# Six products of two units for each output tile in the projections that add to the residual stream, and a wider gap between the halves of their input

## The chip, the cores and the metric

The kernel runs on one core of a Trainium2 chip. The metric is the time of one execution on the device in microseconds (us), taken as the median over several runs. TensorE is called PE below, its weight loads PEld, VectorE DVE, ScalarE ACT, GpSimd POOL, and SyncE SP.

## The reference, cut to what matters

One inference step of a two-layer decoder for two groups of requests that share the weights: a prompt of 256 tokens and 8 sampled tokens, so that every activation has 264 columns. Layer 0 has a Mamba-2 mixer, layer 1 a windowed attention; each is enclosed by two half feed-forwards and followed by a gated embedding.

```python
x = x + 0.5 * swiglu(rmsnorm(x, ffn1_norm), ffn1_wi, ffn1_wo)   # 1024 -> 2816 -> 1024
x = x + mixer_or_attention(rmsnorm(x, mix_norm))                # ends in ssm_out or w_o
x = x + 0.5 * swiglu(rmsnorm(x, ffn2_norm), ffn2_wi, ffn2_wo)
gate = sigmoid(rmsnorm(x, ple_norm) @ ple_gate)
x = x + gate * (p @ ple_proj)
```

## The kernel before, in words

Activations lie transposed: 128 features on the partitions, 264 tokens along the row. The residual stream `x` is 8 such tiles. Every product is made in three parts of a shorter float type: a weight tile is split into `whi` and `wlo`, an activation tile into a high half (`xh`, `hh`) and a low half (`xl`, `hl`), and a product is high weight by high input, high weight by low input, low weight by high input (`split_products`, L503 to L509).

The weights are a list of 369 **units** of 128 x 1024 floats (512 KB), used in order, with a ring of four slots for each of `raw`, `whi` and `wlo`. SP loads unit u + 8 into `raw` once `lo_ready` says that unit u + 4 is split. ACT rounds `raw` to `whi` (L1088) when the slot's last user on PE is done, which `unit_used` tells; DVE makes `wlo` by subtraction (L1563) and raises `lo_ready`; PE waits for `lo_ready` before a unit's first product. In the code of ACT and DVE the call `ahead(stage, i, j)` makes the unit that is four further on than unit j of the stage.

There are two kinds of stages. In an **A stage** (first feed-forward matrix, query, gate, Mamba input) a unit gives one output tile: 24 products into one PSUM bank. In a **B stage** (`f1o0`, `sout`, `f2o0`, `f1o1`, `o`, `f2o1`: the second feed-forward matrix, the Mamba output and the attention output) a unit is one tile of the input, `hh[:, kt, :]` and `hl[:, kt, :]`, for all 8 output tiles: `unit_b` (L744) makes three products into each of the 8 banks in turn, and all banks keep accumulating over the stage. `stage_b` (L779) runs the first unit alone (in `sout` the first three units are done by `sout_part`, in pieces), then a loop of four units a turn, then single units, and the last two units together with six products for each bank, so that the banks become ready one after the other (`b_done`). The feed-forward stages have 22 units, `sout` 16, `o` 8.

At the end of a B stage DVE's `add_b` (L1585) adds the banks to `x` (L1593), ACT's `split_x` (L1132) makes `xh` (L1123) and the squares `sq` (L1126), DVE makes `xl` (L1582), and POOL's `add_squares` (L2189) adds the eight squares one by one, from the second on. PE has gone on with the first two units of the next A stage, `unit_pair` (L544), which waits for `xl` tile by tile and, ahead of the eighth tile, makes the column sums of the squares (L542, in the query stage L539), for which POOL's last addition has to be done. DVE and ACT have orders of their own: ahead of `add_b` DVE makes the `wlo` of the next stage's first two units, units n and n + 1 counted from the B stage's start, which take the slots of units n - 4 and n - 3.

In `sout` DVE's order for j = 0 to 13 is: `wlo` of unit j + 4, then for j = 2 to 9 `normed(j + 6)` (L1961), then for j = 4 to 11 `low_z(j + 4)` (L1945), which is the low half of input tile j + 4. In `f1o1` DVE has the key normalisation (L1721, L1723, L1716) between the `wlo` of units 3 and 4.

Of the kernel before, what the change touches and what calls it, by code (L numbers as in the profile page):

```python
# [22 lines left out]
P = 128  # L23
D = 1024
KT = D // P
T = 256
SEQS = 8
N = T + SEQS
# [8 lines left out]
RING = 4  # L37
UNIT = KT * P
HALF = UNIT // 2
WARM = 30  # L40
PAD = 16
LOW = FT * N + PAD
SCALE = 64 ** -0.5

# [4 lines left out]
U0 = {}  # L49
# [118 lines left out]
def trunk_kernel(nc, weights, xT, g1, pT, cst, vec, convst, ssm0, kcT, vc_in, ck, cv,  # L168
# [3 lines left out]
    with ExitStack() as ctx:  # L172
# [322 lines left out]
        def _(pe):  # L495
# [8 lines left out]
            def split_products(out, w, tile, rh, rl, start, stop):  # L504

                c = slice(tile * P, tile * P + P)
                pe.matmul(out, whi[:, w, c], rh, start=start, stop=False)  # L507
                pe.matmul(out, whi[:, w, c], rl, start=False, stop=False)  # L508
                return pe.matmul(out, wlo[:, w, c], rh, start=False, stop=stop)  # L509
# [234 lines left out]
            def unit_b(stage, u, s, kt, where, order, first, hready):  # L744
# [22 lines left out]
                    mm = split_products(bank[m][:, 0:N], s, m, rh, rl, first, False)  # L767
                mm.then_inc(unit_used, 1)

            def sout_part(j, tiles, last=False):  # L770

                pe.wait_ge(lo_ready, U0["sout"] + j + 1)
                pe.wait_ge(hl_ready, HREADY["sout"] + j + 1)
                for m in tiles:
                    mm = split_products(bank[m][:, 0:N], (U0["sout"] + j) % RING, m, hh[:, j, :], hl[:, j, :], j == 0, False)
                if last:
                    mm.then_inc(unit_used, 1)

            def stage_b(stage, n, after, begun=0):  # L779
# [4 lines left out]
                    begun = 1  # L784
                loops = (n - 2 - begun) // RING
                with pe.Fori(0, loops) as i:
                    for j in range(begun, RING + begun):
                        u, _, s = unit(U0[stage], i, j)
                        unit_b(stage, u, s, i * RING + j, after, range(8), False, i * RING + (h0_ + j + 1))
                for j in range(begun + loops * RING, n - 2):  # L790
                    u, _, s = unit(U0[stage], 0, j)
                    unit_b(stage, u, s, j, after, range(8), False, h0_ + j + 1)

                pe.wait_ge(lo_ready, U0[stage] + n)
                pe.wait_ge(hl_ready, h0_ + n)
                for m in range(KT):
                    for j in (n - 2, n - 1):
                        mm = split_products(bank[m][:, 0:N], (U0[stage] + j) % RING, m, hh[:, j, :], hl[:, j, :], False, j == n - 1)
                    if m < KT - 1:
                        mm.then_inc(b_done, 1)  # L800
                mm.then_inc(unit_used, 2)

            def embed(stage, layer):

# [1758 lines left out]
```

## Time and profile before

| | |
|---|---|
| median of 3 runs | 1190.88 us (1190.69 to 1191.04) |
| the profiled execution's own time | 1190.14 us |
| its span, first to last instruction | 1188.3 us |
| PE busy | 1179.1 us, 99% of the span, 9769 matmuls |
| PE weight loads busy | 1152.0 us, 97% |
| DVE busy | 869.6 us, 73% |
| ACT busy | 699.6 us, 59% |
| POOL busy | 248.3 us, 21% |
| granted TensorE clock | 1.00, the higher of its two levels |

A matmul's row gives its start and the time to its modelled end, about 0.28 us, but the next one starts after about 0.12 us, since they are pipelined. So what a product costs is read from the starts of the first of one stretch and the first of the next, divided by the count, not from the busy time.

### The profile page before, as it was taken

To read this page: it belongs to the slowest core of one execution; us is meant where nothing else is said; L and a number is where in the kernel's file an instruction comes from. 1 tells how busy PE (TensorE), PEld (TensorE's weight loads), DVE (VectorE), ACT (ScalarE), POOL (GpSimd) and SP (SyncE) were. 2 spreads that over 40 slices of the span, in tenths; PEclk is the share of its full clock that TensorE was granted. 3 is DMA by queue.
4 is the path that set the end of the run, shared out by engine and by line. 5 is a ranking of instruction groups with operands and counts; after the bars stand their busy time and mean duration, and the time that the engine had idled before them with its cause. 6 is when DMAs were issued, how large, how long until landed. Compare 5 with 4: busy or idle time off the path is not lost.

```text
span 1188.3 us, 26506 instructions
## 1 busy us (share of the span) xinstructions
PE 1179.1 (99%) x9769; PEld 1152.0 (97%) x9769; DVE 869.6 (73%) x1377; ACT 699.6 (59%) x1149; POOL 248.3 (21%) x352
## 2 busy tenths in 40 slices
PE   9999999999999999999999999999999999999998
PEld 8999999998989899999999999999999899999998
DVE  7767646999899768686745987788468877676448
ACT  6454435787786647555546765555368765444345
POOL 1000002412222202132354333232026310000001
PEclk9999999999999999999999999999999999999999
DMA  8765554755446375877887577656743346555552
GB/s 288 263 198 184 183 177 142 265 185 194 156 148 196 103 224 185 316 225 252 277 292 245 208 271 273 228 170 234 261 155 108 103 164 210 183 184 182 177 180 87
DMA packets 63297, 239.90 MB, mean 202 GB/s; under 512 B 7672, under 2 KB 9632, under 8 KB 58848
## 3 DMA queue, kind: packets, MB, share of 16 engines
q1 hardware_dynamic: 56880, 197.83, 49.9%
q0 software_dynamic: 6064, 40.66, 9.4%
q8 instruction: 41, 0.67, 0.2%
q10 hardware_dynamic: 288, 0.54, 0.2%
q14 instruction: 24, 0.20, 0.0%
HBM read 226.87 MB, written 13.39 MB: 202 GB/s over the span
## 4 chain that ended last, share of the span: by engine, by line
PE 93%; DVE 4%; ACT 1%; issue 1%; DMA 0%; POOL 0%; SPq 0%; DVEq 0%; ACTq 0%; POOLq 0%
PE bank L507 29%; PE bank L508 29%; PE bank L509 29%; PE bank L877 1%; PE bank L872 1%; DVE wlo L1563 1%; DVE xl L1582 1%; PE bank L900 1%; ACT whi L1088 0%; DMA raw<-weights 0%; PE bank L929 0%; ACT under L1481 0%; PE bank L685 0%; PE bank L671 0%; PE bank L886 0%
## 5 line engine op out<-in xcount | busy, mean ns | idle before, releaser
L1563 DVE TENSOR_TENSOR wlo<-raw,whi 128x1024 fp32r<-128x1024 f32 x367 | 457.9, 1251 | 235.4 <-ACT whi L1088 234.0
L507 PE MATMUL bank<-xh,whi 128*128 128x264 f32 x2008 | 576.1, 287 | 1.4 <-DVE xl L1767 0.6
L508 PE MATMUL bank<-xl,whi 128*128 128x264 f32 x2008 | 569.2, 283 | 0.0
L509 PE MATMUL bank<-xh,wlo 128*128 128x264 f32 x2008 | 568.8, 283 | 0.0
L1088 ACT ACTIVATE whi<-raw 128x1024 fp32r<-128x1024 f32 x367 | 385.5, 1055 | 241.1 <-PE bank L509 224.3
L507 PEld LDWEIGHTS bank<-xh,whi 128*128 128x128 f32 x2008 | 378.3, 188 | 5.2 <-issue 2.1
L508 PEld LDWEIGHTS bank<-xl,whi 128*128 128x128 f32 x2008 | 378.4, 188 | 0.9
L509 PEld LDWEIGHTS bank<-xh,wlo 128*128 128x128 f32 x2008 | 376.6, 188 | 0.0
L507 PE MATMUL bank<-hh,whi 128*128 (+1 forms) x896 | 255.3, 285 | 0.0
L509 PE MATMUL bank<-hh,wlo 128*128 (+1 forms) x896 | 254.7, 284 | 0.0
L508 PE MATMUL bank<-hl,whi 128*128 (+1 forms) x896 | 254.4, 284 | 0.0
L507 PEld LDWEIGHTS bank<-hh,whi 128*128 128x128 f32 x896 | 169.0, 189 | 1.2 <-issue 0.8
L508 PEld LDWEIGHTS bank<-hl,whi 128*128 128x128 f32 x896 | 169.0, 189 | 0.1
L509 PEld LDWEIGHTS bank<-hh,wlo 128*128 128x128 f32 x896 | 168.6, 188 | 0.0
L1154 ACT ACTIVATE hh<-gu 128x264 fp32r<-128x264 f32 (+1 forms) x88 | 37.4, 425 | 170.1 <-DVE gu L1622 170.1
L2189 POOL TENSOR_TENSOR sq<-sq 128x264 f32<-128x264 f32 x49 | 39.7, 811 | 447.7 <-ACT sq L1126 442.4
L1610 DVE TENSOR_TENSOR gu<-bank,rstd 128x264 f32<-128x264 f32 x192 | 81.9, 428 | 15.6 <-PE bank L509 13.0
L1627 DVE TENSOR_TENSOR hl<-gu,hh 128x264 f32 (+1 forms) x88 | 42.6, 484 | 28.7 <-ACT hh L1154 28.7
L2338 POOL TENSOR_TENSOR xact<-xact,da_bc 128x512 f32<-128x512 f32 x32 | 38.2, 1195 | 100.5 <-PE bank L509 93.1
L1837 DVE SCALAR_TENSOR_TENSOR xact<-under,vs,xact 128x256 f32<-128x256 f32 x96 | 47.3, 492 | 2.3
L1622 DVE TENSOR_TENSOR gu<-gu 128x264 f32<-128x264 f32 x88 | 44.1, 501 | 0.0
L2343 POOL TENSOR_TENSOR xact<-xact 128x512 f32<-128x512 f32 x20 | 31.6, 1579 | 57.7 <-PE bank L509 53.9
(333 smaller groups left out, 1009.5 us busy)
## 6 DMA issues: line engine op xcount, KB each, us to landing
raw<-weights SPq DMA_DIRECT2D x367, 512.0 KB, 3.6
under<-ssm POOLq DMA_DIRECT2D x8, 1024.0 KB, 6.5
xact<-ssm POOLq DMA_DIRECT2D x8, 1024.0 KB, 7.6
out_ssm_s<-xact POOLq DMA_DIRECT2D x8, 1024.0 KB, 5.8
xact<-dtx_rows POOLq DMA_DIRECT2D x5, 1024.0 KB, 10.7
zs<-dtx_rows POOLq DMA_DIRECT2D x2, 1024.0 KB, 15.0
x<-xT SPq DMA_DIRECT2D x4, 264.0 KB, 5.2
xact<-stat_rows POOLq DMA_DIRECT2D x2, 528.0 KB, 6.4
```

The lines of the kernel that those rows point to most:

```text
L507: pe.matmul(out, whi[:, w, c], rh, start=start, stop=False)
L508: pe.matmul(out, whi[:, w, c], rl, start=False, stop=False)
L509: return pe.matmul(out, wlo[:, w, c], rh, start=False, stop=stop)
L1088: act.activation(whi[:, s, :], raw[:, s, :], ACT.Copy).then_inc(hi_ready, 1)
L1154: act.activation(dst, gu[:, 2 * p + 1, :], ACT.Copy).then_inc(hh_ready, 1)
L1563: dve.tensor_tensor(wlo[:, s, :], raw[:, s, :], whi[:, s, :].bitcast(F32), ALU.subtract).then_inc(lo_ready, 1)
L1610: dve.tensor_tensor(dst, src[:, 0:N], rstd[:, :], ALU.mult).then_inc(a_free, 1)
L1622: dve.tensor_tensor(gu[:, 2 * p + 1, :], gu[:, 2 * p, :], gu[:, 2 * p + 1, :], ALU.mult).then_inc(h_ready, 1)
L1627: dve.tensor_tensor(one(hl), gu[:, 2 * p + 1, :], one(hh).bitcast(F32), ALU.subtract).then_inc(hl_ready, 1)
L1837: dve.scalar_tensor_tensor(out=out, in0=xr[:, k:k + T], scalar=vs[:, V_CW + CT * k + c:V_CW + CT * k + c + 1], in1=out, op0=ALU.mult, op1= ...
L2189: pool.tensor_tensor(sq3[:, 0, :], sq3[:, 0, :], sq3[:, m, :], ALU.add).then_inc(sq_pair, 1)
L2338: pool.tensor_tensor(by_head(part), by_head(part), da_bc[:, 2 * k:2 * k + 2, 4 * q:4 * q + 4].unsqueeze(3).to_broadcast([P, 2, 4, 64]), AL ...
```

## The change

`pair_b` takes two units at once: it waits until the second of them is split and both input tiles are there, makes six products for each of the 8 banks (high weights by both high tiles, high weights by both low tiles, low weights by both high tiles) and hands back both slots with the last product (`unit_used` by 2). `stage_b` uses it two times a turn of its loop, for the rest of the units, and for the last two; where the rest is odd, one unit of the old kind comes first. In a feed-forward stage the order is unit 0, pairs 1-2 to 15-16, unit 17, pairs 18-19 and 20-21; in `sout` pairs 3-4 to 9-10, unit 11, pairs 12-13 and 14-15; in `o` unit 0, pairs 1-2 and 3-4, unit 5, pair 6-7. `PAD`, the number of floats between `hh` and `hl`, goes from 16 to 32, so all tiles that are allocated after it lie 64 bytes further on. Nothing else changes; on DVE, ACT, POOL and SP the instructions and their order are the same.

```diff
--- before.py
+++ after.py
@@ -38,7 +38,7 @@
 UNIT = KT * P
 HALF = UNIT // 2
 WARM = 30
-PAD = 16
+PAD = 32
 LOW = FT * N + PAD
 SCALE = 64 ** -0.5
 
@@ -767,6 +767,25 @@
                     mm = split_products(bank[m][:, 0:N], s, m, rh, rl, first, False)
                 mm.then_inc(unit_used, 1)
 
+            def pair_b(u, s, kt, hready, last=False):
+
+                pe.wait_ge(lo_ready, u + 2)
+                pe.wait_ge(hl_ready, hready)
+                hidden = (lambda t, j: t[:, kt + j, :]) if isinstance(kt, int) else (
+                    lambda t, j: t[:, bass.ds(kt + j, 1), :].rearrange("p a n -> p (a n)"))
+                highs, lows = [hidden(hh, j) for j in range(2)], [hidden(hl, j) for j in range(2)]
+                for m in range(KT):
+                    c = slice(m * P, m * P + P)
+                    for j in range(2):
+                        pe.matmul(bank[m][:, 0:N], whi[:, (s + j) % RING, c], highs[j], start=False, stop=False)
+                    for j in range(2):
+                        pe.matmul(bank[m][:, 0:N], whi[:, (s + j) % RING, c], lows[j], start=False, stop=False)
+                    for j in range(2):
+                        mm = pe.matmul(bank[m][:, 0:N], wlo[:, (s + j) % RING, c], highs[j], start=False, stop=last and j == 1)
+                    if last and m < KT - 1:
+                        mm.then_inc(b_done, 1)
+                mm.then_inc(unit_used, 2)
+
             def sout_part(j, tiles, last=False):
 
                 pe.wait_ge(lo_ready, U0["sout"] + j + 1)
@@ -784,21 +803,17 @@
                     begun = 1
                 loops = (n - 2 - begun) // RING
                 with pe.Fori(0, loops) as i:
-                    for j in range(begun, RING + begun):
+                    for j in range(begun, RING + begun, 2):
                         u, _, s = unit(U0[stage], i, j)
-                        unit_b(stage, u, s, i * RING + j, after, range(8), False, i * RING + (h0_ + j + 1))
-                for j in range(begun + loops * RING, n - 2):
+                        pair_b(u, s, i * RING + j, i * RING + (h0_ + j + 2))
+                rest = begun + loops * RING
+                if (n - rest) % 2:
+                    u, _, s = unit(U0[stage], 0, rest)
+                    unit_b(stage, u, s, rest, after, range(8), False, h0_ + rest + 1)
+                    rest += 1
+                for j in range(rest, n, 2):
                     u, _, s = unit(U0[stage], 0, j)
-                    unit_b(stage, u, s, j, after, range(8), False, h0_ + j + 1)
-
-                pe.wait_ge(lo_ready, U0[stage] + n)
-                pe.wait_ge(hl_ready, h0_ + n)
-                for m in range(KT):
-                    for j in (n - 2, n - 1):
-                        mm = split_products(bank[m][:, 0:N], (U0[stage] + j) % RING, m, hh[:, j, :], hl[:, j, :], False, j == n - 1)
-                    if m < KT - 1:
-                        mm.then_inc(b_done, 1)
-                mm.then_inc(unit_used, 2)
+                    pair_b(u, s, j, h0_ + j + 2, j == n - 2)
 
             def embed(stage, layer):
 
```

On PE, at the entry of `sout`'s loop, the order before is this (the loop begins at the branch; `bank`, `hh` and `whi` are the program's names, and a row is one instruction or several alike):

```order
L507 MATMUL bank<-hh,whi 128x264 [waits hl_ready,lo_ready]
L508 MATMUL bank<-hl,whi 128x264
L509 MATMUL bank<-hh,wlo 128x264
L786 UNCONDITIONAL_BRANCH
L786 ISA
L746 REGISTER_ALU [waits lo_ready]
L507 ISA [waits hl_ready]
L507 MATMUL bank<-hh,whi 128x264
L508 REGISTER_ALU
L508 MATMUL bank<-hl,whi 128x264
L509 MATMUL bank<-hh,wlo 128x264
```

And this is the same place after the change:

```order
L509 MATMUL bank<-hh,wlo 128x264
L805 UNCONDITIONAL_BRANCH
L805 ISA
L773 REGISTER_ALU [waits lo_ready]
L780 ISA [waits hl_ready]
L780 MATMUL bank<-hh,whi 128x264
L780 ISA
L780 MATMUL bank<-hh,whi 128x264
L782 REGISTER_ALU
L782 MATMUL bank<-hl,whi 128x264
L784 MATMUL bank<-hh,wlo 128x264 x2
```

The one wait on `lo_ready` ahead of the first product now asks for unit 4 of the stage, where it asked for unit 3.

On PE, at the seam between the last pair of `f1o0` and the A stage behind it, the changed order is this:

```order
L780 MATMUL bank<-hh,whi 128x264 x2
L782 MATMUL bank<-hl,whi 128x264 x2
L784 MATMUL bank<-hh,wlo 128x264 x2
L507 MATMUL bank<-xh,whi 128x264 [waits b_free,lo_ready,a_free,xl_ready]
L508 MATMUL bank<-xl,whi 128x264
```

Before, it was this:

```order
L507 MATMUL bank<-hh,whi 128x264
L508 MATMUL bank<-hl,whi 128x264
L509 MATMUL bank<-hh,wlo 128x264
L507 MATMUL bank<-xh,whi 128x264 [waits b_free,lo_ready,a_free,xl_ready]
L508 MATMUL bank<-xl,whi 128x264
```

The last pair's products are regrouped, and what waits behind them is the same; the slots of the two units ahead of that pair are handed back together, where it was one by one.

## Rows read from the trace of the kernel before

**Rows 1.** The page, the chain that ended last: share of the span by engine.
```profile
PE 93%; DVE 4%; ACT 1%; issue 1%; DMA 0%; POOL 0%; SPq 0%; DVEq 0%; ACTq 0%; POOLq 0%
```

**Rows 2.** Stretches: us, PE busy (matmuls that touch it), clock, DMA share, GB/s.
```profile
137.13:201.29 64.16, 64.16 (x530) 1.00 0.56 180
464.94:581.02 116.08, 116.08 (x964) 1.00 0.75 262
581.02:586.86 5.84, 5.84 (x51) 1.00 0.74 252
```

**Rows 3.** PE in time: start us, us, what; first products of units 4, 5, 7, 8 of f1o0.
```profile
148.78 0.29 PE L507 MATMUL bank<-hh,whi 128*128 x1
...
151.75 0.28 PE L507 MATMUL bank<-hh,whi 128*128 x1
...
157.58 0.29 PE L507 MATMUL bank<-hh,whi 128*128 x1
...
160.47 0.28 PE L507 MATMUL bank<-hh,whi 128*128 x1
```

**Rows 4.** PE in time: last pair of f1o0 and the next stage; two transposes; warm-up.
```profile
195.47 0.29 PE L507 MATMUL bank<-hh,whi 128*128 128x264 f32 x1
...
201.29 0.28 PE L507 MATMUL bank<-xh,whi 128*128 128x264 f32 x1
...
301.56 0.27 PE L849 MATMUL bank<-cs,xact 128*128 128x128 f32 x1
301.67 0.27 PE L850 MATMUL bank<-cs,xact 128*128 128x128 f32 x1
...
1.28 5.54 PE L502 MATMUL bank<-hh 128*128 128x264 f32 x30 [1.28 <-DVE hh L1761]
```

**Rows 5.** A unit handed back at 186.72, from PE over ACT to DVE.
```profile
186.72 0.28 PE L507 MATMUL bank<-hh,whi 128*128 128x264 f32 x1
...
186.92 1.06 ACT L1088 ACTIVATE whi<-raw 128x1024 fp32r<-128x1024 f32 x1 [1.86 <-PE bank L509]
...
188.01 1.23 DVE L1563 TENSOR_TENSOR wlo<-raw,whi 128x1024 fp32r<-128x1024 f32 x1 [1.69 <-ACT whi L1088]
```

**Rows 6.** Entry of sout's loop: PE's unit 3, ACT's and DVE's unit 4.
```profile
414.83 0.28 PE L507 MATMUL bank<-hh,whi 128*128 x1
...
414.39 2.96 ACT L1088 ACTIVATE whi<-raw 128x1024 fp32r<-128x1024 f32 x3 [2.29 <-PE bank L509]
...
415.48 1.23 DVE L1563 TENSOR_TENSOR wlo<-raw,whi 128x1024 fp32r<-128x1024 f32 x1 [1.55 <-ACT whi L1088]
```

**Rows 7.** sout: PE's unit 10 begins, then DVE makes unit 13 and tile 13.
```profile
435.27 0.29 PE L507 MATMUL bank<-hh,whi 128*128 x1
...
436.62 1.23 DVE L1563 TENSOR_TENSOR wlo<-raw,whi 128x1024 fp32r<-128x1024 f32 x1 [0.96 <-ACT whi L1088]
...
438.17 0.43 DVE L1945 TENSOR_TENSOR hl<-zs,hh 128x264 fp32r<-128x264 f32 x1
```

**Rows 8.** f1o1: PE's unit 3 begins, and DVE makes unit 4.
```profile
826.46 0.28 PE L507 MATMUL bank<-hh,whi 128*128 x1
...
825.43 1.78 DVE L1563 TENSOR_TENSOR wlo<-raw,whi 128x1024 fp32r<-128x1024 f32 x1
```

**Rows 9.** The seam behind f1o0: DVE, POOL, PE.
```profile
196.76 1.22 DVE L1563 TENSOR_TENSOR wlo<-raw,whi 128x1024 fp32r<-128x1024 f32 x1 [1.69 <-ACT whi L1088]
197.90 0.42 DVE L1593 SCALAR_TENSOR_TENSOR x<-bank,x 128x264 f32<-128x264 f32 x1
...
200.00 6.22 POOL L2189 TENSOR_TENSOR sq<-sq 128x264 f32<-128x264 f32 x7 [147.07 <-ACT sq L1126]
...
206.46 0.61 PE L542 MATMUL bank<-sq,cs 128*128 128x264 f32 x2
```

**Rows 10.** The seam behind sout: POOL's additions, then PE's product over them.
```profile
451.56 6.21 POOL L2189 TENSOR_TENSOR sq<-sq 128x264 f32<-128x264 f32 x7 [34.60 <-ACT sq L1126]
...
457.88 0.44 PE L542 MATMUL bank<-sq,cs 128*128 128x264 f32 x1
```

## The prediction

> **What bounds the kernel now.** I read four views. The chain of work that ended last comes first: PE has 93% of it [rows 1], so any time in which PE stands still lengthens the run, and any time that a product saves shortens it. Next, the stretches of a B stage, an A stage and the embedding product between them [rows 2]: the clock is 1.00 throughout, PE has work all the time, and DMA is busy a half to three quarters, so nothing starves. Dividing by the products gives their real price: `f1o0` 64.16 us / 528 = 121.5 ns, the first matrix of the next feed-forward 116.08 / 960 = 120.9 ns, the embedding 5.84 / 48 = 121.7 ns (the counts in the rows hold a few products more that only touch the stretch). Third, PE in order of time, unit by unit [rows 3]: the price is not one number, for unit 4 takes 151.75 - 148.78 = 2.97 us (123.8 ns a product) and unit 7 160.47 - 157.58 = 2.89 us (120.4 ns), with the same kinds of products and banks, and another input tile. Last, who makes what PE waits for, in time, at the places where the change alters a wait [rows 5 to 10].
>
> **What the change does, part by part.** It removes no product. It regroups 98 units: 20 in each of the four feed-forward stages, 12 in `sout`, 6 in `o`; 98 x 24 = 2352 products. It adds two kinds of waiting: a pair begins only when its second unit is split and its second input tile is there, and the first unit's slot is handed back a unit (2.9 us) later.
>
> *The handing back.* From the first product behind the handed-back unit, ACT starts 0.20 us later and takes 1.06, and DVE starts 1.29 us after it and takes 1.23, so a unit is ready 2.52 us after [rows 5]. Of two units handed back together the second `wlo` starts 1.14 us after the first, because that is what the next instruction on DVE does (196.76 to 197.90, [rows 9]); it is ready after 1.29 + 1.14 + 1.23 = 3.66 us. The next pair takes PE 48 x 121.5 ns = 5.8 us, so inside the loops 2.2 us of cover are left and nothing is lost. Where one unit stands alone (unit 17, in `sout` 11), the pair behind it needs only the first of the two: 2.52 us against 2.92, which holds by 0.4. SP's queue is released by the same `lo_ready` at most 2.9 us later, and loads are eight units ahead: nothing. POOL's later work waits on `unit_used` too, up to 2.9 us more for every other piece, and is off PE's path: nothing. If ACT or DVE were held up by 2 us in a loop, that cover would be gone and PE would wait for the rest.
>
> *A wait at the entry of `sout`'s loop.* PE begins unit 3 at 414.83; pair 3-4 has to wait for unit 4, whose slot PE had in use until 414.1 to 414.4, so that ACT starts at 414.39 and DVE ends at 415.48 + 1.23 = 416.71 [rows 6]. Between a release and PE's product lie 0.11 us (POOL's end at 451.56 + 6.21 = 457.77, product at 457.88 [rows 10]). So PE starts at 416.82: **+2.0 us**. Queued behind it on PE is the whole rest of the run.
>
> *The wait at pair 12-13 of `sout`.* It needs input tile 13, whose low half DVE makes behind unit 13's `wlo` and one more instruction. Today PE begins unit 10 at 435.27, thereby handing back unit 9, and that half is done at 438.17 + 0.43 = 438.60 [rows 7]: 3.33 us. After the change unit 9 comes back when unit 11 begins, and unit 11 alone, 2.9 us, is the cover: 3.33 + 0.11 - 2.91 = **+0.5 us**. Pair 9-10 needs tile 10 behind two such rounds, but has a pair's 5.8 us of cover: nothing.
>
> *The wait at pair 3-4 of `f1o1`.* PE begins unit 3 at 826.46; DVE, late from the key normalisation, has unit 4 ready at 825.43 + 1.78 = 827.21 [rows 8]. 827.32 - 826.46 = **+0.9 us**. The first pairs of `f2o0` and `o` have the next thinnest cover; I count nothing there.
>
> *The seams behind the B stages.* This is the largest term. With 22 units (and with 16) units n - 4 and n - 3 are one pair, so both slots come back when the last pair begins, T = 195.47 in `f1o0` [rows 4]. DVE makes the next stage's units n and n + 1 from these slots before `add_b`. Today it has only n + 1 left by then and starts `add_b` at 197.90, which is T + 2.43 [rows 9]. After the change it has both: T + 1.29 + 1.14 + 1.14 = T + 3.57, that is 1.14 us later. `xh`, the squares and `xl` all hang on this, and POOL's seven additions follow the second square without a gap: 200.00 + 6.22 = 206.22 today, 207.36 then [rows 9]. PE's column sums stand right behind them, at 206.46, and would start at 207.47: +1.0. Behind `sout` the sums already wait today (457.77 to 457.88 [rows 10]), so all 1.14 us show. The seams of `f2o0`, `f1o1` and `f2o1` are built alike, and I take 1.07 for each. In `o` units 4 and 5 are not a pair (unit 5 stands alone), so its seam stays. Sum: 1.0 + 1.1 + 3 x 1.07 = **+5.4 us**. What comes late next are the roots and the takes of the A stage's first units; they shift by the same 1.14 us as PE does, so they add nothing.
>
> *The products themselves.* The new order alternates two input tiles, and with 128 bytes between the halves the low tiles lie 64 bytes off their high ones in every block of 256 bytes. No stage of the trace has this order; bounds from rows: the slowest unit 123.8 ns (+2.3 x 2352 = +5.4 us), the fastest 120.4 (-1.1 x 2352 = -2.6 us). Nearest are today's last pair, which already makes six products for each bank from two tiles, (201.29 - 195.47) / 48 = 121.3 ns [rows 4], the embedding 121.7 and the A stage 120.9 [rows 2]. I take 121.2: -0.3 x 2352 = **-0.7 us**. Fewer bank changes are part of that: an A stage changes banks once in 24 products, a B stage once in three, and they differ by 0.6 ns, so halving the changes is worth less than 1.4 us. The Trainium skill speaks for a larger gain there: TensorE: Matmul & The Clock Gate, section "A second HAM failure mode: psum-queue depth-cycling", holds that cycling through PSUM banks makes PE idle briefly again and again. The trace doesn't agree to that extent, with its 0.6 ns and a clock at 1.00.
>
> The sum: 2.0 + 0.5 + 0.9 + 5.4 - 0.7 = +8.1 us. Made against the profiled execution's own 1190.14 us this is 1198.2; that execution lies 0.74 us under the median shown, so on the median's scale it is **1199.0 us**.
>
> **The rivals.** *The products shorten and PE ends faster than before.* The place is the interplay of a product's reads with the next weight load; the change would have to bring the 2352 products from 121.5 down by more than 8.8 / 2352 = 3.7 ns, to under 117.8. For it: two transposes with loads of their own start 0.11 us apart [rows 4], and the price does depend on the input tile [rows 3], which is what the gap between the halves alters. At 114 ns, midway: -17.6 + 8.8 = -8.8 us, 1182.1 us. Against it: no unit in rows 3 and no stage in rows 2 is under 120.4 ns, whatever tiles it mixes. The Trainium skill, same page, section "Back-to-back issue gap", would give 264 / 2.4 + 2.5 = 112.5 ns for such a product, an estimate by which 9 ns could still be had; the rows show none of it. SBUF — State Buffer, section "Who interferes with whom", says that PE's two read ports are independent, by which the gap would do nothing; rows 3 speak against that. Chance 0.07.
>
> *No difference.* The products come down to between 118.8 and 116.8 ns, and the waits eat it: within 2.4 us of today, 1190.9. Chance 0.07.
>
> *More than forecast.* After 2 us of standing still at `sout`'s entry the clock falls to its lower level. The warm-up, which ran mostly at that level, took 5.54 - 0.28 = 5.26 us for 29 starts [rows 4], where 121.5 ns each would make 3.5: some 1.7 us. Or the products come out like a slow unit's, 122.5 ns: +2.4 instead of -0.7. Together 1199.0 + 4.8 = 1203.8, either alone about 1201 to 1202. Chance 0.12.
>
> *The seams cost less*, because PE's sums have more room than the rows tell, or the second `wlo` is overtaken: without that term +2.7, 1193.6 us. Chance 0.08.
>
> **How the numbers follow.** The forecast has the rest, 0.66, with its own range of 1197 to 1201 (a product between 120.7 and 122.0 ns, and half a microsecond on the waits). The range of 8 in 10 goes from 1194.5 to 1202.5. About 0.2%, 2.4 us, is what a measurement of this kernel can tell from no change: faster 0.07, within it 0.07, slower 0.86.
>
> **What would show it.** In the profile after: PE waiting for `wlo` (L1563) at the entry of `sout`'s loop for about 2 us and in `f1o1` for 0.9, for `hl` (L1945) in `sout` once for 0.5; the column sums (L542, L539) waiting for POOL at five seams for about 1 us each and not behind `o`; DVE's `add_b` beginning 3.6 us after the last pair instead of 2.4; `f1o0` at 528 products in about 64.0 us. It would be wrong if those waits are missing, or if a B stage takes under 62.2 us (117.8 ns a product), which would carry the run below today's.

## The result, and the profile after

The changed kernel takes **1203.67 us** (median of 5 executions, 1202.24 to 1205.70) against 1190.88 (1190.52 to 1192.33) before, measured beside it: 1.0106 times as long, 95% interval 1.0095 to 1.0116. Forecast were 1199.0 us and a range up to 1202.5. The sign and most of the places were right; the size was not, and the median lies above the range.

The profiled execution took 1202.24 us, its span 1200.4, which is 12.1 us over the span of before. In the page, the chain of work that ended last [rows 1] now reads:

```profile
PE 77%; DVE 9%; issue 6%; ACT 5%; POOL 1%; DMA 0%; DVEq 0%; SPq 0%; POOLq 0%; ACTq 0%
```

PE's share of the chain has fallen from 93% to 77%, since the chain now runs through DVE (9% for 4%), ACT (5% for 1%) and the path between them (`issue`, 6% for 1%) at the places where PE waits. That is where the chain runs, not time lost: the run is 1% longer. PE's waits, by what ended them (us in total, times, longest):

```profile
PE bank L780 <- DVE wlo L1578: 3.4, 3, 1.9
PE bank L542 <- POOL sq L2204: 1.5, 3, 0.5
...
PE bank L507 <- DVE xl L1597: 1.0, 1, 1.0
PE bank L542 <- issue: 0.5, 1, 0.5
...
PE bank L539 <- POOL sq L2204: 0.5, 1, 0.5
...
PE bank L780 <- DVE hl L1960: 0.4, 1, 0.4
```

(Behind line 800 all numbers are 15 higher than before: `wlo` L1563 is now L1578, `add_b` L1593 is L1608, POOL's L2189 is L2204.) Line 780 is the first product of a pair, L542 and L539 are the column sums at the seams. One wait more for `wlo` than forecast is there, and one at L507 for `xl`. The stretches of the six B stages, as [rows 2], in the columns us, PE busy, PEld, DVE, ACT, POOL, clock, DMA share, GB/s:

```profile
137.02:201.30 64.28, 64.28 (x530) 64.28 (x529) 28.26 (x31) 24.77 (x28) 0.18 (x1) 1.00 0.52 173
411.54:456.89 45.35, 43.02 (x350) 42.60 (x349) 26.58 (x38) 21.64 (x30) 2.05 (x4) 1.00 0.57 174
592.08:658.39 66.31, 64.72 (x530) 64.31 (x529) 39.10 (x33) 32.21 (x47) 31.41 (x27) 1.00 0.74 264
826.01:891.64 65.63, 64.75 (x531) 64.52 (x530) 33.28 (x33) 25.83 (x31) 4.36 (x6) 1.00 0.62 211
955.34:978.84 23.50, 23.50 (x192) 23.50 (x193) 13.96 (x18) 12.59 (x18) 1.10 (x2) 1.00 0.60 205
1106.96:1171.25 64.29, 64.29 (x530) 64.29 (x529) 28.26 (x31) 24.78 (x28) 0.19 (x1) 1.00 0.52 174
```

Taking the whole run apart at the first product of each B stage and at the first product behind it gives this account of the 12.1 us. The seams lie in the second column, whose last row goes up to PE's last product.

| | B stage, before → after | from its end up to the next B stage, before → after |
|---|---|---|
| start | | 137.13 → 137.02: -0.1 |
| f1o0 | 64.16 → 64.29: +0.1 | 209.08 → 210.24: +1.2 |
| sout | 42.41 → 45.34: +2.9 | 134.08 → 135.20: +1.1 |
| f2o0 | 64.16 → 66.31: **+2.2** | 166.53 → 167.62: +1.1 |
| f1o1 | 64.33 → 65.63: +1.3 | 62.60 → 63.70: +1.1 |
| o | 23.43 → 23.51: +0.1 | 128.12 → 128.12: 0 |
| f2o1 | 64.16 → 64.29: +0.1 | 23.63 → 24.65: +1.0 |

Second column: +5.5 us in five seams and none behind `o`, where 5.4 and none were forecast. One seam in time, as [rows 9], DVE, POOL and PE:

```profile
196.75 2.36 DVE L1578 TENSOR_TENSOR wlo<-raw,whi 128x1024 fp32r<-128x1024 f32 x2 [4.65 <-ACT whi L1103]
199.02 0.77 DVE L1608 SCALAR_TENSOR_TENSOR x<-bank,x 128x264 f32<-128x264 f32 x2
...
201.12 0.77 POOL L2204 TENSOR_TENSOR sq<-sq 128x264 f32<-128x264 f32 x1 [148.31 <-ACT sq L1141]
...
207.42 0.68 PE L542 MATMUL bank<-sq,cs 128*128 128x264 f32 x2 [0.55 <-issue]
```

DVE now makes two `wlo` where it made one, and `add_b` begins at 199.02 instead of 197.90: 1.12 us later, POOL 1.12 later too. The entries of the loops in `sout` and `f1o1` [rows 6, 8] and the wait for tile 13 [rows 7], each with PE's first product behind the wait (`x1` at L780) and the DVE row that ended it:

```profile
416.67 2.36 DVE L1578 TENSOR_TENSOR wlo<-raw,whi 128x1024 fp32r<-128x1024 f32 x2 [1.59 <-ACT whi L1103]
...
418.14 0.39 PE L780 MATMUL bank<-hh,whi 128*128 x1 [1.95 <-DVE wlo L1578]
...
444.52 0.43 DVE L1960 TENSOR_TENSOR hl<-zs,hh 128x264 fp32r<-128x264 f32 x1
...
445.10 0.36 PE L780 MATMUL bank<-hh,whi 128*128 128x264 f32 x1 [0.38 <-DVE hl L1960]
...
833.91 1.78 DVE L1578 TENSOR_TENSOR wlo<-raw,whi 128x1024 fp32r<-128x1024 f32 x1
...
835.93 0.39 PE L780 MATMUL bank<-hh,whi 128*128 x1 [0.88 <-DVE wlo L1578]
```

From the start of the last product ahead of the wait to the first behind it are 2234, 667 and 1155 ns, where products follow each other in about 120; the product after that comes 0.2 us later instead of 0.12. So the terms are 2.2, 0.6 and 1.1 us; forecast were 2.0, 0.5 and 0.9. In `f1o1` the row of `wlo` ends at 833.91 + 1.78 = 835.69 and PE starts at 835.93: 0.24 us from a release to the product, where the prediction took the 0.11 of a seam. In `sout` it is 0.25 (the first of the two `wlo` ends at 417.89 in the trace), at tile 13 0.15.

What was not forecast is `f2o0`. During this stage POOL works on the Mamba states of the sampled tokens in pieces of 512 columns, four multiplications and then four additions for each token (`late_piece`), and each piece is released by a unit that PE hands back. In time, POOL, DVE and PE at its pair 18-19:

```profile
642.96 1.30 POOL L2358 TENSOR_TENSOR xact<-xact 128x512 f32<-128x512 f32 x1
...
643.07 2.27 DVE L1578 TENSOR_TENSOR wlo<-raw,whi 128x1024 fp32r<-128x1024 f32 x1 [2.65 <-ACT whi L1103]
...
645.40 0.39 PE L780 MATMUL bank<-hh,whi 128*128 128x264 f32 x1 [0.59 <-DVE wlo L1578]
```

and at its end:

```profile
652.73 3.50 DVE L1578 TENSOR_TENSOR wlo<-raw,whi 128x1024 fp32r<-128x1024 f32 x2 [4.02 <-ACT whi L1103]
...
652.88 2.27 POOL L2358 TENSOR_TENSOR xact<-xact 128x512 f32<-128x512 f32 x1
...
653.93 2.30 DVE L1578 TENSOR_TENSOR wlo<-raw,whi 128x1024 fp32r<-128x1024 f32 x1
656.16 0.76 DVE L1608 SCALAR_TENSOR_TENSOR x<-bank,x 128x264 f32<-128x264 f32 x2
...
658.39 0.36 PE L507 MATMUL bank<-xh,whi 128*128 128x264 f32 x1 [1.00 <-DVE xl L1597]
```

A `wlo` that takes 1.23 us elsewhere takes 2.3 where it meets one of POOL's additions, and the late `add_b` keeps PE from the first product of `pg0`, the next A stage (the gate of the embedding). The two waits, 882 and 1284 ns from start to start, make 2.0 of the stage's 2.2 us.

### The profile page after: what moved, and what is told of

Its sections match the earlier page's. It is cut to its first block, busy times and chain, and to the rows that moved or that the text cites. A ratio compares the mean times of both kernels' runs of the same rounds, so it can differ in the third digit from the quotient of the medians.

```text
span 1200.4 us, 26427 instructions
## 1 busy us (share of the span) xinstructions
PE 1184.4 (99%) x9769; PEld 1154.4 (96%) x9769; DVE 870.9 (73%) x1377; ACT 695.0 (58%) x1149; POOL 248.4 (21%) x352
## 4 chain that ended last, share of the span: by engine, by line
PE 77%; DVE 9%; issue 6%; ACT 5%; POOL 1%; DMA 0%; DVEq 0%; SPq 0%; POOLq 0%; ACTq 0%
PE bank L507 17%; PE bank L508 17%; PE bank L509 16%; PE bank L780 7%; PE bank L784 7%; PE bank L782 7%; ACT whi L1103 3%; DVE wlo L1578 3%; POOL sq L2204 1%; DVE gu L1637 1%; DVE gu L1625 1%; PE bank L892 1%; PE bank L887 1%; DVE xl L1597 1%; PE bank L915 1%
## 5 line engine op out<-in xcount | busy, mean ns | idle before, releaser
L1578 DVE TENSOR_TENSOR wlo<-raw,whi 128x1024 fp32r<-128x1024 f32 x367 | 461.4, 1269 | 245.4 <-ACT whi L1103 244.1
L507 PE MATMUL bank<-xh,whi 128*128 128x264 f32 x2008 | 577.0, 287 | 1.7 <-DVE xl L1597 1.0
L1103 ACT ACTIVATE whi<-raw 128x1024 fp32r<-128x1024 f32 x367 | 381.5, 1053 | 261.2 <-PE bank L784 168.6
L507 PEld LDWEIGHTS bank<-xh,whi 128*128 128x128 f32 x2008 | 378.2, 188 | 6.5 <-issue 2.8
L780 PE MATMUL bank<-hh,whi 128*128 (+1 forms) x784 | 159.6, 285 | 3.8 <-DVE wlo L1578 3.4
L784 PE MATMUL bank<-hh,wlo 128*128 (+1 forms) x784 | 159.5, 285 | 0.0
L782 PE MATMUL bank<-hl,whi 128*128 (+1 forms) x784 | 159.0, 284 | 0.0
L2204 POOL TENSOR_TENSOR sq<-sq 128x264 f32<-128x264 f32 x49 | 39.8, 811 | 452.6 <-ACT sq L1141 447.3
L780 PEld LDWEIGHTS bank<-hh,whi 128*128 128x128 f32 x784 | 121.4, 188 | 4.6 <-issue 3.8
L784 PEld LDWEIGHTS bank<-hh,wlo 128*128 128x128 f32 x784 | 121.7, 189 | 0.0
L782 PEld LDWEIGHTS bank<-hl,whi 128*128 128x128 f32 x784 | 121.4, 188 | 0.0
L1642 DVE TENSOR_TENSOR hl<-gu,hh 128x264 f32 (+1 forms) x88 | 39.6, 450 | 28.7 <-ACT hh L1169 28.7
```

What stands on the lines that cost most here:

```text
L780: pe.matmul(bank[m][:, 0:N], whi[:, (s + j) % RING, c], highs[j], start=False, stop=False)
L782: pe.matmul(bank[m][:, 0:N], whi[:, (s + j) % RING, c], lows[j], start=False, stop=False)
L784: mm = pe.matmul(bank[m][:, 0:N], wlo[:, (s + j) % RING, c], highs[j], start=False, stop=last and j == 1)
L1103: act.activation(whi[:, s, :], raw[:, s, :], ACT.Copy).then_inc(hi_ready, 1)
L1578: dve.tensor_tensor(wlo[:, s, :], raw[:, s, :], whi[:, s, :].bitcast(F32), ALU.subtract).then_inc(lo_ready, 1)
L2204: pool.tensor_tensor(sq3[:, 0, :], sq3[:, 0, :], sq3[:, m, :], ALU.add).then_inc(sq_pair, 1)
```

## The experiments

All times are compared with runs of the kernel before on the same chip (medians 1190.55 to 1191.13 us). Stage times are read as in the table above.

### The order at the seam

```diff
-                if (n - rest) % 2:
+                while rest < n:
                     u, _, s = unit(U0[stage], 0, rest)
-                    unit_b(...)
-                    rest += 1
-                for j in range(rest, n, 2):
-                    pair_b(u, s, j, h0_ + j + 2, j == n - 2)
+                    if rest == n - 3:
+                        unit_b(stage, u, s, rest, after, range(8), False, h0_ + rest + 1)
+                        rest += 1
+                    else:
+                        pair_b(u, s, rest, h0_ + rest + 2, rest == n - 2)
+                        rest += 2
```

> The changed kernel with one edit: behind its loop a stage takes a pair first and its single unit third from the end, so that units n-4 and n-3 are handed back apart, as before. Theory (the joint hand-back makes VectorE late at the seam): the five seams give back about 5.3 us, and because the pair that follows a single unit is then the last one, so do the wait for tile 13 in sout (0.6), the wait inside f2o0 (0.9) and the late last residual sum behind f2o0 (1.2, with its work on POOL beside it): 1194.3 profiled, median about 1195. What stays is the loop entry of sout (2.2), of f1o1 (1.1) and the products (0.6). If the gaps inside f2o0 have nothing to do with which units are handed back together, it stays at about 1197.5. Rival (the time is in the order of the products, not in the hand-back): over 1200.

Measured: 1198.08 us (1196.62 to 1199.28), 1.0058 [1.0044, 1.0071], 3 us over the expected median. The parts between the stages are back at 209.09, 134.03, 62.58 and 23.58 us: four of the five seams are gone, and nothing but which units are taken and handed back together was touched there, so the joint hand-back is shown as their cause. The waits for tile 13 and at pair 18-19 are gone too. But the fifth seam stays, 167.66 us behind `f2o0`, and `f2o0` takes 64.66, with a gap of 538 ns at its end. The rows say why, though no run tests it: the pair 17-18 still comes back at once, and three of POOL's additions in a row stretch both of the last `wlo`, so that `add_b` starts 4.1 us after the last pair (at 650.24), though its two units came back apart.

```profile
647.55 5.76 POOL L2359 TENSOR_TENSOR xact<-xact 128x512 f32<-128x512 f32 x3 [3.51 <-PE bank L784]
...
649.86 4.54 DVE L1579 TENSOR_TENSOR wlo<-raw,whi 128x1024 fp32r<-128x1024 f32 x2
654.32 0.76 DVE L1609 SCALAR_TENSOR_TENSOR x<-bank,x 128x264 f32<-128x264 f32 x2
```

That is 1.5 of the 3.8 us by which the profiled execution lies over the expected 1194.3. The rest, and 0.5 us that other parts gained, lies in two things: its first B stage began 1.1 us later (138.09), for which no row gives a reason, and `sout` took 46.42 us, longer than in the changed kernel. The stretches of `sout`, from the wait on (same columns as above):

```profile
415.78:418.02 2.24, 0.29 (x4) 0.08 (x2) 1.48 (x2) 2.24 (x3) 1.41 (x3) 1.00 0.24 82
418.02:419.37 1.35, 1.35 (x10) 1.35 (x11) 1.35 (x2) 0.39 (x1) 0.00 (x0) 0.97 0.56 84
419.37:422.67 3.30, 3.30 (x17) 3.30 (x16) 0.67 (x1) 0.00 (x0) 0.00 (x0) 0.50 0.97 169
422.67:425.00 2.33, 2.33 (x20) 2.33 (x20) 0.49 (x1) 0.00 (x0) 0.00 (x0) 0.99 1.02 415
```

The granted clock halves, to 1.2 GHz, some 1.3 us after the wait has ended, and 15 products follow each other at 220 ns. In the profiled execution of the changed kernel it doesn't, behind the same wait:

```profile
419.50:422.80 3.30, 3.30 (x30) 3.30 (x28) 0.66 (x1) 0.00 (x0) 0.00 (x0) 1.00 0.96 166
```

### The order of the products, and the gap

Three kernels. The second experiment keeps waits and hand-back of the pair and puts the products of before between them:

```diff
-                for m in range(KT):
-                    ...
+                    for j in range(2):
+                        for m in range(KT):
+                            mm = split_products(bank[m][:, 0:N], (s + j) % RING, m, highs[j], lows[j], False, False)
                 mm.then_inc(unit_used, 2)
```

> The changed kernel with the products inside a pair in the order of before (all eight banks for one unit, then for the other), but with the pair's waits ahead of it and its hand-back behind it. Theory (waits and hand-back carry the loss, the product order some 0.6 us): 1201.5 profiled, median within 1 us of the changed kernel (1203 +-1), all gaps at their places. Rival (six products into one bank, with changed input tiles, cost more each, and a product in the old order is 121.5 ns): the same gaps, but the stages' mean product goes from 121.75 back to 121.5 ns, which is the 0.6 us. Second rival (the order is what costs): under 1197.

The third is the changed kernel with `PAD = 16`, the fourth the kernel before with `PAD = 32`.

> The changed kernel with 16 numbers (64 bytes) between hh and hl as before. Theory (a product's time goes by the place of its own input tile, in a cycle of eight tiles, and each tile is read equally often): no difference, within 0.6 us of the changed kernel. If the wider gap helped the pairs, this one is slower by up to 1.5 us; if the wider gap is what made the products 121.75 ns where before had 121.5, it is faster by 0.6 us.

> The kernel before with 128 bytes between hh and hl and nothing else. Theory: no difference (1190.9 +-0.6), the mean product 121.5 ns as before, but the low products take the place in the cycle that their shifted start gives them (two tiles of the eight further on). Rival (the gap itself costs or gives): over 1191.6 or under 1190.2.

Measured: 1203.46 us (1202.79 to 1204.77), 1202.71 (1201.88 to 1204.43) and 1191.62 (1191.34 to 1193.66). The second has every wait of the changed kernel at its place, four of them within 0.03 us of its length and the one in `f1o1` 0.17 us longer: the loss is in waits and hand-back, not in the order. The price of the products is under what medians can tell and is read from `f1o0`, where no kernel waits. Its stretch in the second, third and fourth experiment:

```profile
137.66:201.99 64.33, 64.33 (x530) 64.33 (x529) 28.29 (x31) 24.79 (x28) 0.20 (x1) 1.00 0.52 173
```

```profile
139.31:203.34 64.03, 64.03 (x530) 64.03 (x529) 28.32 (x31) 24.84 (x29) 0.25 (x1) 1.00 0.52 174
```

```profile
137.72:202.06 64.34, 64.34 (x531) 64.34 (x530) 30.23 (x34) 26.92 (x31) 1.19 (x2) 1.00 0.55 180
```

Four profiled executions of kernels with the same `f1o0` as the changed one give 64.286 or 64.287 us, so differences of this size can be read. Of what a B stage's products read, the gap moves `hl` alone. With before (64.16) and the changed kernel (64.29) this is a table of two by two: at 64 bytes unit by unit 64.16, in pairs 64.04; at 128 bytes 64.33 and 64.29. So the pairs do help, by 0.12 and 0.04 us a stage, and the wider gap takes 0.17 and 0.25. My "no difference" for the gap is refuted by the stage times of both experiments on it (the medians can hardly tell: 1191.62 is 0.5 us over before, with an interval of 0.9996 to 1.0014), and so is "back to 121.5 ns" in the second: the gap has a price of its own, and at 128 bytes the old order costs 64.33 / 528 = 121.8 ns.

### POOL's additions

```diff
-                    pool.tensor_tensor(part, part, late_b(q)[:, cols], ALU.add).then_inc(late_sum, 1)
+                    wide = 32 if U0["f2o0"] <= late_unit(n) < U0["f2o0"] + FT else 512
+                    pool.tensor_tensor(part[:, 0:wide], ..., ALU.add).then_inc(late_sum, 1)
```

This kernel leaves out most of those sums.

> The changed kernel, in which POOL's additions for the late outputs are 32 columns wide instead of 512 during f2o0 (most of those sums are left out, all else stays). Theory A (the pair hands two units back at once, POOL then has two additions in a row, the second beside VectorE's low parts, and those take 2.2 us instead of 1.2 while it lasts): low parts of 1.2 us all through f2o0, its gaps of 0.88 us at pair 18-19 and 1.28 us at the first product behind it both under 0.3 us, stage 64.3 us instead of 66.3. The gap of 0.8 us behind the first unit of pg0 stays. Theory B (ScalarE's scaling of late outer products between the two high parts of a pair delays the second low part): gaps and stage stay within 0.3 us of the changed kernel's.

Measured: 1201.81 us (1200.78 to 1202.74), 1.0092 [1.0077, 1.0108]. Pair 18-19 and the end of the stage:

```profile
643.76 0.26 POOL L2359 TENSOR_TENSOR xact<-xact 128x32 f32<-128x32 f32 x1
...
643.86 1.23 DVE L1578 TENSOR_TENSOR wlo<-raw,whi 128x1024 fp32r<-128x1024 f32 x1 [2.66 <-ACT whi L1103]
...
653.81 1.22 DVE L1578 TENSOR_TENSOR wlo<-raw,whi 128x1024 fp32r<-128x1024 f32 x1
654.94 0.77 DVE L1608 SCALAR_TENSOR_TENSOR x<-bank,x 128x264 f32<-128x264 f32 x2
```

`f2o0` takes 64.29 us, neither gap is there, and ScalarE still scales its outer products between the two high parts. Theory A holds for the gaps, B falls; but not every `wlo` of the stage is back at 1.2 us: of 22, three still take 2.0 to 2.2 and one 1.5, beside POOL's multiplications, which were left as they were and cost PE nothing here. The seam behind `f2o0` stays (167.62), now an ordinary one. The rows also say how the two engines share. At 642.96 POOL began first and took its usual 1.30 us, and DVE took 2.27, about its own 1.23 and what was left of POOL's; at 652.88 POOL came second and took 2.27, and DVE's next one, which came third, 2.30. They take turns, they don't share. The Trainium skill says so of two inputs in SBUF against a GpSimd instruction that reads SBUF: the second to issue blocks until the first is done (SBUF — State Buffer, "Who interferes with whom"). The trace agrees. In the kernel before, at the end of the stage, the addition (1.29 us) started 0.24 us after the hand-back and the `wlo` 1.11 us after the addition, so that they overlapped by 0.2 us and the `wlo` took 1.27; in pairs there are two of each in a row. The sharing itself could be seen before the change, in the middle of the same stage, where it cost PE nothing:

```profile
619.18 2.05 POOL L2343 TENSOR_TENSOR xact<-xact,zs 128x512 f32<-128x512 f32 x1 [1.61 <-PE bank L509]
...
620.29 2.02 DVE L1563 TENSOR_TENSOR wlo<-raw,whi 128x1024 fp32r<-128x1024 f32 x1 [0.22 <-ACT whi L1088]
```

### The entries

```diff
                     begun = 1
+                if stage in ("sout", "f1o1"):
+                    u, _, s = unit(U0[stage], 0, begun)
+                    unit_b(stage, u, s, begun, after, range(8), False, h0_ + begun + 1)
+                    begun += 1
                 loops = (n - 2 - begun) // RING
...
-                    if rest == n - 3:
+                    if rest == n - 3 or rest == n - 4:
```

> The kernel of the first experiment (single unit third from the end) with unit 3 of sout and unit 1 of f1o1 on their own ahead of the loops, so that their first pairs are 4-5 and 2-3, and the two units behind the loops of these stages are single. Theory: the wait of 2.2 us in sout goes, and the half-rate products behind it with it (1.5 us in that run), the wait of 1.1 us in f1o1 goes; sout takes 42.6 us, f1o1 64.5; time 1198.1 - 5 = 1193 +-0.7, and its executions lie within 1.5 us of each other, where those of the changed kernel are 3.5 apart. Rival (the low parts are late in any order at a loop's entry, and the wait moves to the next pair): sout over 43.5 us and a gap of over 0.8 us at pair 4-5.

Measured: 1194.05 us (1193.70 to 1195.89), 1.0029 [1.0018, 1.0040]. `f1o1` has no gap left (64.61), as expected. In `sout` the wait of 2.2 us became two, of 445 ns at pair 4-5 and 1055 at pair 6-7, and the stage takes 43.97 us: here the rival was half right. So the median lies over the expected 1193.7, and the executions lie 2.2 us apart, not 1.5. The second wait in the profile (the first, shorter one counts as `issue` there):

```profile
PE bank L780 <- DVE wlo L1583: 0.8, 1, 0.8
```

No half-rate products appear behind either in the profiled execution.

### Stages put back

The changed kernel with `f2o0` alone in the stage code of before, unit by unit, and in the other kernel `sout` alone:

```diff
+                if stage == "f2o0":
+                    ...
+                    return
                 loops = (n - 2 - begun) // RING
```

> The changed kernel with f2o0 alone in the order of before (unit by unit). Theory: f2o0 goes from 66.3 to 64.3 us and the gap of 0.8 us behind the first unit of pg0 goes, 3.0 us together: 1203.7 - 3.0 = 1200.7 +-0.8 (the executions differ by what happens behind the wait in sout). Rival (the wait in front of pg0 comes from the stage's place and not from pairs): the gap of 1.28 us at its end stays over 0.6 us.

> The changed kernel with sout alone in the order of before (unit by unit). Theory: in the profiled execution of the changed kernel sout and the seam behind it cost 2.9 and 1.1 us, and in other executions the products behind the wait of 2.2 us run at half rate for 1.1 to 1.6 us; with no wait there, no half-rate stretch and no scatter. Stage 42.5 us, time 1203.7 - 4.0 - 1.5 = 1198.2 +-0.7, executions within 1.5 us of each other. Rival (scatter and the extra 1.4 us of the median come from elsewhere): 1199.7, still over 3 us between executions.

Measured: 1202.54 us (1201.76 to 1202.63) and 1198.83 (1198.19 to 1200.36). `f2o0` is at 64.33 with 166.51 behind it, 3.1 us less in all, as expected. The median is not: it fell by 1.1 us and lies 1.0 over the expected range. Half-rate products in `sout` hide part of the gain in the profiled execution (46.84 us, with a mean granted clock of 0.998), and the other three executions have 0.996. With `sout` in units it takes 42.53 us with 134.06 behind it, 4.0 less, and the median fell by 4.8. The executions lie 2.2 us apart, not the 1.5 expected; the mean granted clock of all five is 0.999 or 1.000.

### Everything mended

The entries' kernel with `f2o0` in units and `PAD = 16`, and the same with `sout` in units as well:

> The kernel e6_entries with f2o0 unit by unit as in e7_f2o0_in_units, and 64 bytes between hh and hl. Theory (every loss was a hand-back or an entry, and six products into one bank are worth 0.2 ns each at that gap, 121.3 for 121.5 ns): stages at or below those of before (64.04 us for 64.16), 1190.9 - 0.5 = 1190.4, within 0.2% of before. Rival (pairs cost something else that the gaps do not show): 1192 or more.

> The kernel e8_all_mended with sout, too, unit by unit; 64 bytes between hh and hl; pairs in f1o0, f1o1, o and f2o1, with no joint hand-back of n-4 and n-3. Theory: sout back at 42.4 us (from 43.9), f1o0 and f2o1 at 63.9 (64.16 before), f1o1 at 64.3 and f2o0 at 64.16 as before: 0.5 us less than before, 1190.4; a tie within the measurement's 0.2%. Rival (something of the pair is left that the gaps do not show): 1191.6 or more.

Measured: 1191.89 us (1190.88 to 1193.75), 1.0010 [1.0000, 1.0019], and **1190.46** (1189.78 to 1192.77), 0.9996 [0.9987, 1.0005]. The first misses its 1190.4 and still pays for `sout` (43.92 us). The second has no wait on the B stages' units that before hasn't, and its stages are:

```profile
138.16:202.08 63.92, 63.92 (x530) 63.92 (x529) 29.41 (x34) 25.91 (x31) 1.19 (x2) 1.00 0.55 180
411.12:453.54 42.42, 42.42 (x350) 42.42 (x350) 27.88 (x40) 23.10 (x33) 3.02 (x5) 1.00 0.62 195
587.61:651.77 64.16, 64.16 (x530) 64.16 (x529) 32.41 (x35) 34.38 (x50) 29.58 (x28) 1.00 0.81 279
818.34:882.65 64.31, 64.31 (x530) 64.28 (x529) 34.44 (x36) 27.09 (x34) 5.42 (x7) 1.00 0.66 220
```

Its gain, 0.24 us in `f1o0` and `f2o1` each and 0.1 in `o`, is 0.6 us, which the measurement can't tell from nothing. Of the 0.24 us the pairs make 0.12, as above; the other half came with the new place of the single unit, and why is open.

### Where the place of a tile comes in

```diff
+        sb("ahead_of_under", [P, 32])
         with nc.sbuf_tensor("under", [P, 2 * FT * N + PAD], F32) as under:
```

> The kernel before with 128 bytes laid ahead of hh and hl, both moved by as much and the gap between them as before; nothing else. Theory (the products' cycle of 2.88 to 2.96 us per unit goes by where a tile lies, 1056 bytes each, so that the place repeats every eight tiles, and not by its number or by the bank): the slow units 4 and 12 of f1o0 (2964 ns) become units 0, 8 and 16 and the fast ones 7 and 15 (2885 ns) become 3, 11 and 19, the stage stays at 64.2 +-0.1 us and the time at 1190.9 +-0.6. Rival (the cycle belongs to the order of units, or to the moving part's distance from the weights' other stream): units 4 and 12 stay the slow ones.

Measured: 1190.99 us (1190.00 to 1191.32), 0.9999 [0.9990, 1.0008]; `f1o0` takes 64.20. From the first product of a unit to the first of the next, units 0 to 7, in ns: before 2904, 2929, 2904, 2915, **2964**, 2922, 2911, **2885**; moved by 128 bytes **2963**, 2922, 2911, **2885**, 2916, 2925, 2901, 2915. From there on both repeat every eight, and the moved kernel's units 0 to 7 are the units 4 to 11 of before (2964, 2922, 2911, 2885, 2916, 2925, 2902, 2915) to within 1 ns. The order moved by four, as the theory has it.

### The wait by itself

The kernel before, with one line:

```diff
+                if stage == "sout":
+                    pe.wait_ge(lo_ready, U0[stage] + begun + 2)
                 loops = (n - 2 - begun) // RING
```

> The kernel before with one added wait and nothing else: at the entry of sout's loop PE waits until unit 4 is split, as the pair 3-4 of the changed kernel does. Theory: PE stands still for about 2 us, sout takes 44.5 to 44.7 us instead of 42.4 where the clock holds, and in part of the executions (in four of six profiled ones with this wait so far) the clock halves for 3.3 us behind it and costs 1.1 to 1.6 more: executions in two groups, about 1193.1 and 1194.5, median 1194 +-0.8. Rival (the wait is all, and the changed kernel's scatter has another cause): 1193.1, executions within 1 us of each other.

Measured: 1194.40 us (1192.92 to 1196.18), 1.0032 [1.0022, 1.0042], where 13 executions of before beside it lay within 1.6 us. One wait costs 3.8 us in the median, of which the wait itself is 2.5: it was 2532 ns long here, 0.3 more than in the changed kernel.

```profile
415.01 0.28 PE L509 MATMUL bank<-hh,wlo 128*128 128x264 f32 x1
417.54 0.38 PE L507 MATMUL bank<-hh,whi 128*128 x1 [2.25 <-DVE wlo L1565]
...
415.77 2.36 DVE L1565 TENSOR_TENSOR wlo<-raw,whi 128x1024 fp32r<-128x1024 f32 x2 [1.59 <-ACT whi L1090]
```

DVE starts 0.76 us after PE's last product in both kernels, so the 0.3 us lie behind the `wlo`. The added wait stands ahead of the loop, and in the trace PE's sequencer starts the loop (L788) at 417.04 and 417.22, after it; in the changed kernel the wait stands inside the loop.

Nine executions spread over 3.3 us, and the mean granted clock on record for each sorts them: 1192.92 and 1193.32 us at 1.000, four from 1194.15 to 1194.57 at 0.998, three from 1195.52 to 1196.18 at 0.997. A stretch of 3.4 us at half the clock takes 0.0014 off the mean of such a run (an estimate, 3.4 / 2 / 1192), so these are executions with none, one and two of them, about 1.4 us apart. The profiled one kept its clock in `sout` (45.04 us) and lost it ahead of `o`, where no wait was added:

```profile
940.00:945.00 5.00, 4.75 (x75) 4.09 (x71) 3.95 (x13) 3.63 (x15) 0.00 (x0) 1.00 0.01 3
945.70:949.00 3.30, 3.30 (x24) 2.97 (x23) 2.70 (x7) 0.78 (x3) 0.00 (x0) 0.50 0.45 159
```

There the part from `f1o1` to `o` takes 63.75 us instead of 62.60. The scatter came with the wait, in three groups and not in the two that I expected, and it goes with the clock. Why a stretch so far behind the wait is hit is open: the same thing happened in one other profiled execution, of the kernel with all but `sout` mended.

## Why the prediction failed in size, point by point

*The bound.* Right: PE has all of the time, and each of its waits shows in full.

*The seams, 5.4 us.* Right in mechanism, place and size: 5.5, with none behind `o`. (The rounded terms in the prediction add up to 5.3; 5.4 is their sum with 1.01 and 1.14.) The first experiment takes four of the five away by one change of order.

*The entries and tile 13, 2.0 + 0.5 + 0.9.* Right in place, small in size: 2.2 + 0.6 + 1.1. `wlo` was ready when the rows said, within 0.04 us; but PE's product started 0.24 us behind it where I had taken 0.11, and the second product behind a wait also comes late (220 ns for 120).

*"Which holds by 0.4", and POOL's later work "off PE's path: nothing".* **This is the step that failed.** (Inside the loops nothing was lost, as forecast.) Its place is `f2o0`, and it was 2.0 us where the sum had nothing: 0.86 at the pair behind single unit 17, for which I had 0.4 us of cover, and 1.16 at the end of the stage. I priced the later pieces of POOL by PE's path alone, and did not ask what else runs when two units come back at once. Two of POOL's pieces then stand in a row (at pair 18-19 a multiplication and an addition, at the end two additions) beside two `wlo`, and DVE waits its turn. The sentence on what would be lost if DVE were held up by 2 us named the point, but I put no row beside it, though POOL's 30 us of work in this stage stood in the trace, and in it a `wlo` of 2.02 us. The experiment with short additions shows the cause. Without these 2.0 us the median would lie at about 1201.7 (1203.67 - 2.0), inside the range.

*The products, -0.7 us.* The sign was wrong: +0.7 us, from the stages' remainders (0.13 us in each of four, 0.1 to 0.2 in the others together). I had read the gap as part of what changes the price and then taken the price of the old last pair, at 64 bytes. Pairs alone give -0.1 us a stage, the gap alone +0.2. Had the gap stayed at 64 bytes, 0.12 us over the 480 regrouped products of a stage would be 0.25 ns each, and over 2352 about -0.6 us (an estimate): the -0.7 was right for a kernel that was not the changed one. Of the rival for shorter products: the formula behind its 112.5 ns is one that the Trainium skill gives for a single matmul by itself, and it says in the same section that a stream of weight loads and matmuls has another spacing (TensorE: Matmul & The Clock Gate, "Back-to-back issue gap"), so that it was no price for these products; the stages of the kernel before took 120.9 to 121.8 ns.

*The median.* The profiled execution of the changed kernel is its fastest; its median lies 1.4 us above. In the forecast that difference was that of before, 0.7 us. Half-rate products behind `sout`'s wait, fifteen at 0.1 us too much each, appeared in four of seven profiled executions that have that wait in full (with them: seam order, order of before, gap of 64 bytes, `f2o0` in units; without: the changed kernel, short additions, the wait by itself), and putting `sout` back took 4.8 us off the median where its parts of the profiled execution are 4.0 shorter. The other executions of the changed kernel left no trace, but their mean granted clocks are on record: 0.999 for 1202.24, 1202.81 and 1204.13 us, 0.998 for 1203.67, 0.997 for 1205.70. Two of the three slow ones fit the clock and one doesn't, so that this is where the 1.4 us lie is shown only in part. The rival "more than forecast" had the clock and priced it at 1.7 us, near the 1.5 of such a stretch; its 1203.8 is the median's number, but by luck: 3.1 of its 4.8 us were slow products, of which 1.4 came, and it had no `f2o0`.

Sum of the profiled execution: 5.5 + 3.9 + 2.0 + 0.7 - 0.1 for the start = 12.0 of the 12.1 us.

## What to carry to other kernels

Two buffers handed back at once made every engine that waits for them run twice in a row here, all at the same moment: look for pairs of engines that then stand side by side on one resource (here VectorE and POOL), not only for the latency of each. Where a pair must wait for its second half, the first pair of each loop and the last one of each stage decide, and a single unit put third from the end cost nothing and took away nearly half of this loss (5.6 of 12.8 us). A wait of 2 us on TensorE has to be priced with what may follow it at half the clock, as a case of its own, and the profiled execution may be one that was spared.

## What the runs showed of the hardware that was not expected

The time of a product depends on where its input lies. With tiles of 1056 bytes, whose start comes back to the same place in 256 bytes every eight tiles, 24 products take 2885 to 2964 ns in a fixed cycle, the same in every pass; moving the tiles by 128 bytes moves the cycle by four tiles with the same values, and moving only the low halves by 64 bytes makes another cycle that is 0.2 us slower over 528 products. What in the reads causes it, no run tells.

After PE had stood still for 1.95 us, the granted clock halved in four profiled executions and not in two others, for 3.4 us, and only 0.5 to 1.3 us after PE was at work again (0.5, 1.0, 1.3 and 1.3). Twice it halved ahead of `o`, with no added wait in front of it; in the one shown PE had been busy for 4.75 of the 5 us before.
